# A hybrid decoder layer on one core: the 16 memory-projection tiles placed between gate and z tiles instead of in one block

## The chip, the cores and the metric

The kernel runs on one core of a Trainium2 chip. The metric is the device time of one execution in microseconds, as the median of the runs. TensorE (PE in the profile, its weight loads PEld), VectorE (DVE), ScalarE (ACT), GpSimd (POOL) and the DMA queue of SyncE (SP) each run their own stream of instructions in order and wait for one another by semaphores.

## What is computed

One decoder layer over 512 positions of width 1024, in float32. The normalised input `n` goes through one wide projection; its column blocks feed three branches, and sigmoid gates merge them:

```python
n = rms_norm(h, ln_mix_pre[l])
(da_q, da_k, da_v, dn_q, dn_k, dn_v, dn_z, dn_b, dn_a, ca_q, gate_logits) = [
    n @ wp for wp in jnp.split(w_in[l], SPLIT_IDX, axis=-1)]
y_a = diff_attention(...)      # 8 heads, two softmax maps each
y_b = gated delta rule(...)    # 8 heads, convolution of width 4 on q, k, v
mkv = rms_norm(mem, mem_norm_g[l]) @ w_mem_kv[l]
mk, mv = jnp.split(mkv, 2, axis=-1)
y_c = memory_attention(ca_q, mk, mv)   # 4 heads over 256 memory tokens
proj = jnp.einsum('bsiw,iwd->bsid', ys, w_branch[l])
mixed = jnp.sum(gates * proj, axis=2)
h = h + rms_norm(mixed @ w_out[l], ln_mix_post[l])
```

A squared-ReLU MLP follows. The memory projection (`mkv`) has 256 rows instead of 512.

## The kernel before

**Tiles.** Every projection is cut into weight tiles of 1024 x 128 (512 KB). A float32 product is made of three products of split operands: a tile's weights come into `w_raw` by DMA (L623, three buffers), ScalarE makes the high part `w_hi` (L841), VectorE the low part `w_lo` (L1136), three buffers each. TensorE multiplies them (L1541 to L1543) into one of the two banks of `acc`: 24 matmuls of 512 columns for an ordinary tile, 24 of 256 columns for a memory tile `mk` or `mv`. ScalarE evacuates the bank.

**Slots.** `plan_mixing` (L120) lays the first 104 tiles out over 192 slots. A slot holds half an ordinary tile (12 matmuls) or a whole memory tile, and beside it at most one step of the attention chain (`attn_steps`) and one of the delta chain (`delta_steps`). Every engine walks the same list of slots, so each engine's stream is fixed when the kernel is built. On TensorE the order in a slot is: main half, delta step, attention step. On VectorE: delta step, maxima of an attention map, the low part of the tile three ahead of the one that the slot evacuates, the convolution of that tile, the finish of the tile before, the scaling of the map of two slots before, the norm of an attention output. A low part is thus made only in a slot that evacuates a tile:

```python
                if ev is not None:
                    split_lo(ev + SPL)
```

**The order of the tiles** comes from `ORDER` (L81): groups taken one after the other, each as soon as the step that frees its buffers has been planned, and a gate tile where the next group is not free yet. The groups are `conv` n (q, k, v tiles of delta pair n: `dq`, `dk`, `dv`, two heads each, with a convolution), `mem` (all 16 memory tiles), `cq` n (two tiles of the cross queries), `z` n (two tiles `dz`), `head` n (`aq`, `ak`, `av`). The 24 gate tiles write their sigmoid to HBM, after a pass by GpSimd (L771), and the DMA queue stands until that is done.

**The steps.** Delta pair p (0 to 3; two heads, here called pair p): `dq`, `dk`, `dv` transpose the convolved tiles `conv_o` (L1656) once all six tiles of the pair are finished; `dq` and `dk` are followed by norms on VectorE (L1307 to L1313, `dk` also L1328), while GpSimd fills `d_ET` (L742) after `dk`. Then come transposes, decay, products (`dL`, `dA`), a doubling inversion (`Za`, `Wb`, `Tc`), the scan over four chunks (`sa`, `sb`), whose last step has a norm of the state's output `d_LT` (L1353, L1307 to L1313), and the output `dO` (L1362). Cross head h: `cs` (scores), `ct`, `cv` (values; spilled to HBM by the DMA queue). Attention head h: `av`, `as0` and `as1` (the two maps, L1616; bias and maxima on VectorE, L1271 to L1276, exponentials on ScalarE, L964), scaling of both maps on VectorE (L1287 to L1295), `at` (transposes of the scaled map, L1622), `ap` (value product, L1627; norm of the output `o_a` on VectorE, L1299 to L1303), `ay` (transposes of the output). TensorE starts a step of a chain only when the steps before it in the chain are done on ScalarE and VectorE.

After the 192 slots come the branch projections, the output projection and the MLP, 112 further tiles that the change does not touch.

Of the kernel before, what the change touches and what calls it, by code (L numbers as in the profile page):

```python
# [32 lines left out]
KT = D // P  # L33
# [44 lines left out]

ORDER = [("conv", 0), ("mem", 0), ("cq", 0), ("z", 0), ("conv", 1), ("cq", 1), ("cq", 2), ("cq", 3), ("z", 1),  # L81
         ("head", 0), ("head", 1), ("conv", 2), ("head", 2), ("head", 3), ("z", 2), ("head", 4), ("conv", 3),
         ("head", 5), ("head", 6), ("z", 3), ("head", 7)]

# [1 line left out]
def cover(step):  # L86

    last_state = step[0] == "sb" and step[2] == ST - 1
    return COVER.get("sb_last" if last_state else step[0], 1)


def attn_steps():

    out = [("mv", 0), ("mv", 1)]
    for h in range(HC):
        out += [("cs", h), ("ct", h), ("cv", h)]
    for h in range(HA):
        out += [("av", h), ("as0", h), ("as1", h), ("at", h), ("ap", h), ("ay", h)]
    return out


def delta_steps():

    out = []
    for p in range(HB // 2):
        out += [(k, p, 0) for k in ("dq", "dk", "dv", "dE", "dqT", "dqd", "dkT", "dkb", "dL", "dA", "T1")]
        for lv in range(1, NM):
            out += [("Za", p, lv), ("Wb" if lv < NM - 1 else "Wl", p, lv)]
            if lv < NM - 1:
                out.append(("Tc", p, lv))  # L110
        out += [("dU", p, 0), ("dW", p, 0)]
        for c in range(ST):
            if c:
                out.append(("sa", p, c))
            out.append(("sb", p, c))
        out.append(("dO", p, 0))
    return out


def plan_mixing():  # L120

    attn, delta = attn_steps(), delta_steps()
    def group(kind, n):
        return {"mem": [("mk", j) for j in range(KT)] + [("mv", j) for j in range(KT)],
                "conv": [(k, 2 * n + i) for k in ("dq", "dk", "dv") for i in range(2)],
                "z": [("dz", 2 * n + i) for i in range(2)],
                "cq": [("cq", 2 * n + i) for i in range(2)],
                "head": [(k, n) for k in ("aq", "ak", "av")]}[kind]  # L130

    groups = [group(*g) for g in ORDER]
    gates = [("gate", i * KT + m) for i in (2, 0, 1) for m in range(KT)]
    tiles, slots = [], []
    done = {}
    evac = {}
    need_free = {}
    for p in range(1, HB // 2):
        for k in ("dq", "dk", "dv"):
            for i in range(2):  # L140
                need_free[(k, 2 * p + i)] = ("dv", p - 1, 0)
        for i in range(2):
            need_free[("dz", 2 * p + i)] = ("dO", p - 1, 0)
    for j in range(2 * HC):
        need_free[("cq", j)] = ("mv", 1) if j < 4 else ("cs", j // 2 - 2)
    for h in range(HA):
        for k in ("aq", "ak", "av"):
            need_free[(k, h)] = ("cv", HC - 1) if h < 2 else ("as1", h - 2)
    need_tile = {}
    need_tile[("mv", 0)] = need_tile[("mv", 1)] = ("mv", KT - 1)  # L150
    for h in range(HC):
        need_tile[("cs", h)] = ("cq", 2 * h + 1)
    for h in range(HA):
        need_tile[("av", h)] = ("av", h)
    for p in range(HB // 2):
        need_tile[("dq", p, 0)] = ("dv", 2 * p + 1)
        need_tile[("dO", p, 0)] = ("dz", 2 * p + 1)
    ai = di = 0
    a_next = d_next = 0
    finish = {}  # L160
    todo = list(groups)
    now = []
    half = 0
    slot = 0
    while todo or gates or now or ai < len(attn) or di < len(delta) or finish.get(slot):
        if not now:
            if todo and all(need_free.get(t) is None or need_free[t] in done for t in todo[0][:1]):
                now = list(todo.pop(0))
            elif gates:
                now = [gates.pop(0)]  # L170
        main = ev = None
        if now:
            short = now[0][0] in ("mk", "mv")
            main = (len(tiles), None if short else half)
            if half == 1 or short:
                t = now.pop(0)
                tiles.append(t)
                ev = len(tiles) - 1
                evac[t] = slot
                if t[0] in ("dq", "dk", "dv", "dz"):  # L180
                    finish[slot + 1] = ev
                    evac[t] = slot + 1
            half = 0 if short else half ^ 1
        sa = sd = None
        if ai < len(attn) and slot >= a_next:
            t = need_tile.get(attn[ai])
            if t is None or evac.get(t, slot + 9) < slot:
                sa = ai
                done[attn[ai]] = slot
                a_next = slot + cover(attn[ai])  # L190
                ai += 1
        if di < len(delta) and slot >= d_next:
            t = need_tile.get(delta[di])
            if t is None or evac.get(t, slot + 9) < slot:
                sd = di
                done[delta[di]] = slot
                d_next = slot + cover(delta[di])
                di += 1
        slots.append((main, ev, finish.get(slot), sa, sd))
        slot += 1  # L200
    return tiles, slots, need_free


def plan_tiles():

    tiles, slots, need_free = plan_mixing()
    n_mix = len(tiles)
    tiles = list(tiles)
    for i in (2, 0, 1):
        tiles += [("br", i * KT + m) for m in range(KT)]  # L210
    tiles += [("out", m) for m in range(KT)]
    for half in range(2):
        tiles += [("f1", half * 16 + f) for f in range(16)]
        tiles += [("f2", (2 * half + g) * KT + m) for m in range(KT) for g in range(2)]
    return tiles, n_mix, slots, need_free
# [1720 lines left out]
```

## Time and profile before

| | |
|---|---|
| median of 3 runs | 1498.67 us (1494.84 to 1499.0) |
| the profiled execution | 1497.8 us |
| its span | 1496.0 us, mean granted clock 0.982 |
| TensorE matmul busy | 1432.0 us, 96% of the span |
| TensorE weight loads | 1200.0 us, 80% |
| VectorE busy | 773.1 us, 52% |
| ScalarE busy | 482.7 us, 32% |
| GpSimd busy | 258.7 us, 17% |
| DMA | 142.77 MB, mean 95 GB/s |

The profile is one execution. Matmuls overlap, so a busy TensorE is not one at its peak, and a matmul's length includes the overlap with the next. An idle time stands before the instruction that it delayed, with the engine and tile whose work ended it. The granted clock is a share of 2.4 GHz; its other level is 0.5, 1.2 GHz.

### The profile page before, as it was taken

The numbers are of one execution on the slowest core, as the hardware profiler recorded it, in microseconds if no ns is written. First come the engines' busy times: TensorE is split into PE (matmuls) and PEld (weight loads), VectorE is DVE, ScalarE is ACT, GpSimd is POOL, SyncE is SP. The second block draws the span as 40 slices with busy tenths as digits, with TensorE's granted clock in tenths as the row PEclk, the third lists the DMA queues.
The fourth block names the chain that finished last, engine by engine and source line by source line (L and its number), as shares of the span: only waits on it lengthen the run. The fifth ranks groups of instructions, "written<-read, shape, count | busy, mean of one in ns | idle before, by whom it ended". The sixth has DMA issues, their size and how long they took to land.

```text
span 1496.0 us, 18535 instructions
## 1 busy us (share of the span) xinstructions
PE 1432.0 (96%) x7540; PEld 1200.0 (80%) x7540; DVE 773.1 (52%) x1243; ACT 482.7 (32%) x762; POOL 258.7 (17%) x180
## 2 busy tenths in 40 slices
PE   5879999989999999999899999999979999999998
PEld 5679878768887778888688888888878888888887
DVE  6775236643367676754765334355355533255333
ACT  4334333333243343343343322111243221122221
POOL 2003210005200013100014231223232210022110
PEclk9989999999999999999999999999989999999998
DMA  5243121213111212102312255554412222323221
GB/s 197 69 163 122 64 85 57 85 43 120 57 52 55 78 38 83 62 31 71 106 50 71 92 164 175 189 184 148 168 54 82 97 87 87 111 85 99 97 86 57
DMA packets 46412, 142.77 MB, mean 95 GB/s; under 512 B 4944, under 2 KB 7416, under 8 KB 46328
## 3 DMA queue, kind: packets, MB, share of 16 engines
q1 hardware_dynamic: 46328, 141.59, 28.0%
q8 instruction: 60, 0.98, 0.3%
q14 instruction: 24, 0.20, 0.0%
HBM read 126.88 MB, written 16.27 MB: 96 GB/s over the span
## 4 chain that ended last, share of the span: by engine, by line
PE 82%; DVE 11%; ACT 3%; DMA 2%; issue 2%; SPq 0%; DVEq 0%; POOL 0%; ACTq 0%
PE acc L1541 21%; PE acc L1543 21%; PE acc L1542 21%; PE ps_d L1670 5%; PE ps_a L1616 2%; PE ps_d L1661 2%; DVE conv_y L1232 2%; PE ps_d L1675 2%; DVE w_lo L1136 2%; DMA w_raw<-weights 2%; ACT w_hi L841 1%; PE ps_a L1606 1%; PE ps_a L1627 1%; PE ps_a L1595 1%; PE ps_d L1664 1%
## 5 line engine op out<-in xcount | busy, mean ns | idle before, releaser
L1541 PE MATMUL acc<-n_hi,w_hi 128*128 128x512 f32 (+1 forms) x984 | 399.8, 406 | 6.7 <-DVE n_lo L1161 4.3
L1136 DVE TENSOR_TENSOR w_lo<-w_raw,w_hi 128x1024 fp32r<-128x1024 f32 x200 | 289.0, 1453 | 190.8 <-ACT w_hi L841 190.5
L1542 PE MATMUL acc<-n_lo,w_hi 128*128 128x512 f32 (+1 forms) x984 | 383.8, 390 | 0.0
L1543 PE MATMUL acc<-n_hi,w_lo 128*128 128x512 f32 (+1 forms) x984 | 383.8, 390 | 0.0
L841 ACT CAST w_hi<-w_raw 128x1024 fp32r<-128x1024 f32 x200 | 209.5, 1047 | 249.2 <-PE acc L1543 232.4
L1541 PEld LDWEIGHTS acc<-n_hi,w_hi 128*128 128x128 f32 x984 | 188.6, 192 | 45.4 <-issue 6.4
L1543 PEld LDWEIGHTS acc<-n_hi,w_lo 128*128 128x128 f32 x984 | 187.8, 191 | 41.1
L1542 PEld LDWEIGHTS acc<-n_lo,w_hi 128*128 128x128 f32 x984 | 188.7, 192 | 35.6 <-issue 1.0
L1543 PE MATMUL acc<-h_hi,w_lo 128*128 128x512 f32 x256 | 101.1, 395 | 0.0
L1541 PE MATMUL acc<-h_hi,w_hi 128*128 128x512 f32 x256 | 101.1, 395 | 0.0
L1542 PE MATMUL acc<-h_lo,w_hi 128*128 128x512 f32 x256 | 101.1, 395 | 0.0
L829 POOL TENSOR_TENSOR h_lo<-sq,h_hi 128x512 fp32r<-128x512 f32 x32 | 41.4, 1294 | 234.2 <-DVE h_hi L1472 234.2
L1541 PE MATMUL acc<-y_hi,w_hi 128*128 128x512 f32 x192 | 76.1, 396 | 0.0
L1543 PE MATMUL acc<-y_hi,w_lo 128*128 128x512 f32 x192 | 76.0, 396 | 0.0
L1542 PE MATMUL acc<-y_lo,w_hi 128*128 128x512 f32 x192 | 76.0, 396 | 0.0
L1081 ACT ACTIVATE sq<-relu 128x512 f32<-128x512 f32 x32 | 20.3, 634 | 126.1 <-DVE relu L1470 126.1
L1543 PEld LDWEIGHTS acc<-h_hi,w_lo 128*128 128x128 f32 x256 | 48.0, 188 | 11.7
L1541 PEld LDWEIGHTS acc<-h_hi,w_hi 128*128 128x128 f32 x256 | 48.0, 188 | 11.7
L1542 PEld LDWEIGHTS acc<-h_lo,w_hi 128*128 128x128 f32 x256 | 48.0, 188 | 11.7
L1232 DVE SCALAR_TENSOR_TENSOR conv_y<-conv_x,par,conv_y 128x512 f32<-128x512 f32 x72 | 54.1, 752 | 2.6
L1670 PEld LDWEIGHTS ps_d<-d_TT,d_KTT 128*128 128x128 f32 x384 | 46.5, 192 | 2.3 <-ACT d_KTT L987 0.3
L1541 PE MATMUL acc<-m_hi,w_hi 128*128 128x256 f32 x128 | 39.3, 307 | 9.1 <-DVE w_lo L1136 5.4
(311 smaller groups left out, 2056.5 us busy)
## 6 DMA issues: line engine op xcount, KB each, us to landing
w_raw<-weights SPq DMA_DIRECT2D x200, 512.0 KB, 3.5
gate_scratch<-gate_st SPq DMA_DIRECT2D x24, 256.0 KB, 2.2
g_in<-gate_scratch SPq DMA_DIRECT2D x24, 256.0 KB, 3.8
y_raw<-y_scratch SPq DMA_DIRECT2D x16, 256.0 KB, 3.6
x_tok<-x SPq DMA_DIRECT2D x4, 512.0 KB, 5.3
y_scratch<-y_st SPq DMA_DIRECT2D x4, 512.0 KB, 3.3
y_scratch<-d_ET SPq DMA_DIRECT2D x4, 512.0 KB, 3.2
y_scratch<-y_st SPq DMA_DIRECT2D x8, 256.0 KB, 2.6
```

What stands on the lines that cost most here:

```text
L829: nc.gpsimd.tensor_tensor(h_lo[:, f % 16], sq[:, f % 2], h_hi[:, f % 16].bitcast(F32), ALU.subtract).then_inc(hl_ok, 1)
L841: nc.scalar.copy(w_hi[:, t % SPL], w_raw[:, t % RAW]).then_inc(hi_ready, 1)
L1081: nc.scalar.activation(sq[:, f % 2], relu[:, f % 2], ACT.Square).then_inc(sq_ok, 1)
L1136: V_.tensor_tensor(w_lo[:, t % SPL], w_raw[:, t % RAW], w_hi[:, t % SPL].bitcast(F32), ALU.subtract).then_inc(lo_ready, 1)
L1232: ins = V_.scalar_tensor_tensor(out=y, in0=conv_x[:, n % 2, j:j + S], scalar=par[:, col + j:col + j + 1], in1=y, op0=ALU.mult, op1=ALU.add)
L1541: mm(bank, wh, hi_of(k), start=start and k == 0, stop=False)
L1542: mm(bank, wh, lo_of(k), start=False, stop=False)
L1543: last = mm(bank, wl, hi_of(k), start=False, stop=stop and k == KT - 1)
L1616: last = mm(ps[:, bank_of[q]:bank_of[q] + (q + 1) * P], qkv_T[rows_m, h % 2, 0, q * P:(q + 1) * P], qkv_T[rows_m, h % 2, 1, 0:(q + 1) * P] ...
L1661: last = nc.tensor.transpose(dst[m], src[:, m], ident)
L1670: last = mm(ps_d[:, 0, m * P // 2:(m + 1) * P // 2], a[:, m], halves(b[:, m], c, second), start=True, stop=True)
L1675: last = mm(dst[m], a[:, m], b[:, m], start=True, stop=True)
```

## The change

`ORDER` now takes the memory tiles two by two, as groups `mem` 0 to 7 (`mk` for 0 to 3, `mv` for 4 to 7). Three gate tiles, which before had no place of their own, are named in `ORDER` between them, and the z group of pair 0 as well; cross queries 0 and 1 come after the convolution tiles of pair 1.

```diff
--- before.py
+++ after.py
@@ -78,7 +78,8 @@
 
 
 
-ORDER = [("conv", 0), ("mem", 0), ("cq", 0), ("z", 0), ("conv", 1), ("cq", 1), ("cq", 2), ("cq", 3), ("z", 1),
+ORDER = [("conv", 0), ("mem", 0), ("gate", 0), ("mem", 1), ("mem", 2), ("gate", 1), ("mem", 3), ("mem", 4),
+         ("z", 0), ("mem", 5), ("mem", 6), ("gate", 2), ("mem", 7), ("conv", 1), ("cq", 0), ("cq", 1), ("cq", 2), ("cq", 3), ("z", 1),
          ("head", 0), ("head", 1), ("conv", 2), ("head", 2), ("head", 3), ("z", 2), ("head", 4), ("conv", 3),
          ("head", 5), ("head", 6), ("z", 3), ("head", 7)]
 
@@ -122,15 +123,18 @@
 
 
     attn, delta = attn_steps(), delta_steps()
+    gates = [("gate", i * KT + m) for i in (2, 0, 1) for m in range(KT)]
+    n_early = sum(kind == "gate" for kind, n in ORDER)
     def group(kind, n):
-        return {"mem": [("mk", j) for j in range(KT)] + [("mv", j) for j in range(KT)],
+        return {"mem": [("mk" if n < KT // 2 else "mv", 2 * n % KT + i) for i in range(2)],
+                "gate": gates[n:n + 1],
                 "conv": [(k, 2 * n + i) for k in ("dq", "dk", "dv") for i in range(2)],
                 "z": [("dz", 2 * n + i) for i in range(2)],
                 "cq": [("cq", 2 * n + i) for i in range(2)],
                 "head": [(k, n) for k in ("aq", "ak", "av")]}[kind]
 
     groups = [group(*g) for g in ORDER]
-    gates = [("gate", i * KT + m) for i in (2, 0, 1) for m in range(KT)]
+    gates = gates[n_early:]
     tiles, slots = [], []
     done = {}
     evac = {}
```

The work of each tile and the number of slots, 192, stay. Where things stand, by slot (each ordinary tile takes two):

| slots | main tiles before | main tiles now |
|---|---|---|
| 12-13 | mk 0, mk 1 | mk 0, mk 1 |
| 14-15 | mk 2, mk 3 | gate 16 |
| 16-19 | mk 4 to mk 7 | mk 2 to mk 5 |
| 20-21 | mv 0, mv 1 | gate 17 |
| 22-25 | mv 2 to mv 5 | mk 6, mk 7, mv 0, mv 1 |
| 26-29 | mv 6, mv 7, gate 16 | dz 0, dz 1 |
| 30-33 | cq 0, cq 1 | mv 2 to mv 5 |
| 34-37 | dz 0, dz 1 | gate 18, mv 6, mv 7 |
| 38-49 | convolution tiles of pair 1 | the same |
| 84-95 | convolution tiles of pair 2 | 90-101 |
| 118-129 | convolution tiles of pair 3 | 124-135 |

All delta steps keep their slots (pair 2: `dq` 103, `dk` 105; pair 3: `dq` 148, `dk` 150; last `sb` of pair 1: 98, its `dO`: 101). The attention steps do not: `cs` of cross heads 0 to 3 moves from slots 34, 54, 60, 66 to 54, 60, 66, 72, and every step of the eight attention heads comes six slots later (`as0`, `as1` of head 1 from 91, 94 to 97, 100; `at`, `ap`, `ay` of head 1 from 98, 99, 101 to 104, 105, 107; `as1` and `at` of head 5 from 142, 146 to 148, 152).

First place: ScalarE at the start of the memory tiles, from the last convolution tile of pair 0 on (`conv_x<-conv_y` is its tanh). `mk_T<-acc` evacuates a memory tile, `gate_st<-acc` a gate tile, `w_hi<-w_raw` is the high part of the tile three ahead, `d_Q<-ps_d` and `d_K<-ps_d` are the copies after the q and k transposes. Before:

```order
L841 CAST w_hi<-w_raw 128x1024
L896 COPY mk_T<-acc 128x256
L841 CAST w_hi<-w_raw 128x1024
L927 ACTIVATE conv_x<-conv_y 128x512
L896 COPY mk_T<-acc 128x256
L841 CAST w_hi<-w_raw 128x1024
L990 COPY d_Q<-ps_d 128x1024
L896 COPY mk_T<-acc 128x256
L841 CAST w_hi<-w_raw 128x1024
L896 COPY mk_T<-acc 128x256
L841 CAST w_hi<-w_raw 128x1024
L990 COPY d_K<-ps_d 128x1024
```

Now:

```order
L845 CAST w_hi<-w_raw 128x1024
L900 COPY mk_T<-acc 128x256
L845 CAST w_hi<-w_raw 128x1024
L931 ACTIVATE conv_x<-conv_y 128x512
L900 COPY mk_T<-acc 128x256
L845 CAST w_hi<-w_raw 128x1024
L994 COPY d_Q<-ps_d 128x1024
L924 ACTIVATE gate_st<-acc 128x512
L845 CAST w_hi<-w_raw 128x1024
L994 COPY d_K<-ps_d 128x1024
L900 COPY mk_T<-acc 128x256
L845 CAST w_hi<-w_raw 128x1024
```

Between the copies of q and k there were two evacuations and two high parts, and now there is one of each, of a gate tile.

Second place: VectorE around the last convolution tile of pair 2. `conv_o` is the finish of a convolution, `ps_a<-ps_a,strip` the bias of an attention map, `state` a step of the scan of pair 1, `d_ET<-ps_d,smd,zs` its output, `w_lo` a low part. Before:

```order
L1136 TENSOR_TENSOR w_lo<-w_raw,w_hi 128x1024
L1230 TENSOR_SCALAR conv_y<-conv_x,par 128x512
L1232 SCALAR_TENSOR_TENSOR conv_y<-conv_x,par,conv_y 128x512 x3
L1353 SCALAR_TENSOR_TENSOR state<-state,e_all,ps_d 128x128 x2
L1246 SCALAR_TENSOR_TENSOR conv_o<-conv_x,conv_y 128x512
L1287 RECIPROCAL smd<-smd 128x8
L1288 TENSOR_SCALAR smd<-smd 128x4
```

Then the rest of a scaling, the last state norm of pair 1, an output norm, and right ahead of the norm of q:

```order
L1127 SCALAR_TENSOR_TENSOR smd<-smd 128x4
L1303 TENSOR_TENSOR o_a<-o_a,smd 128x512
L1362 SCALAR_TENSOR_TENSOR d_ET<-ps_d,smd,zs 128x1024
L1136 TENSOR_TENSOR w_lo<-w_raw,w_hi 128x1024
L1307 TENSOR_TENSOR d_SCR<-d_Q 128x1024
L1308 TENSOR_REDUCE smd<-d_SCR 128x8
```

Now:

```order
L1275 TENSOR_TENSOR ps_a<-ps_a,strip 128x3x256
L1276 TENSOR_TENSOR ps_a<-ps_a,strip 128x128
L1278 TENSOR_REDUCE smd<-ps_a 128x1 x4
L1280 TENSOR_SCALAR smd<-smd 128x4
L1250 SCALAR_TENSOR_TENSOR conv_o<-conv_x,conv_y 128x512
L1366 SCALAR_TENSOR_TENSOR d_ET<-ps_d,smd,zs 128x1024
L1140 TENSOR_TENSOR w_lo<-w_raw,w_hi 128x1024
L1234 TENSOR_SCALAR conv_y<-conv_x,par 128x512
L1236 SCALAR_TENSOR_TENSOR conv_y<-conv_x,par,conv_y 128x512 x3
L1250 SCALAR_TENSOR_TENSOR conv_o<-conv_x,conv_y 128x512
L1291 RECIPROCAL smd<-smd 128x8
```

The last `conv_o` stood ahead of the last state norm; now it comes after that norm, after the second map of head 1 and after the output of pair 1, and only the scaling of head 1's maps (L1291 to L1299) lies between it and the norm of q.

Third place: VectorE between the norms of q and k of pair 3 (`d_SCR<-d_K` begins the latter). Before:

```order
L1312 TENSOR_SCALAR smd<-smd 128x8
L1313 TENSOR_TENSOR d_Q<-d_Q,smd 128x1024
L1136 TENSOR_TENSOR w_lo<-w_raw,w_hi 128x1024
L1307 TENSOR_TENSOR d_SCR<-d_K 128x1024
L1308 TENSOR_REDUCE smd<-d_SCR 128x8
```

Now:

```order
L1316 TENSOR_SCALAR smd<-smd 128x8
L1317 TENSOR_TENSOR d_Q<-d_Q,smd 128x1024
L1275 TENSOR_TENSOR ps_a<-ps_a,strip 128x3x256
L1276 TENSOR_TENSOR ps_a<-ps_a,strip 128x128
L1278 TENSOR_REDUCE smd<-ps_a 128x1 x4
L1280 TENSOR_SCALAR smd<-smd 128x4
L1140 TENSOR_TENSOR w_lo<-w_raw,w_hi 128x1024
L1311 TENSOR_TENSOR d_SCR<-d_K 128x1024
L1312 TENSOR_REDUCE smd<-d_SCR 128x8
```

The bias and maxima of head 5's second map now stand between the two norms, and the scaling of its maps comes behind the norm of k. Line numbers of the changed kernel are four higher.

## Rows read from the trace of the kernel before

**Rows 1.** Stretches: start:end, length, busy PE, PEld, DVE, ACT, POOL (instructions), clock, DMA, GB/s

```profile
70.00:106.00 36.00, 24.50 (x168) 23.45 (x169) 30.00 (x51) 13.71 (x23) 2.78 (x1) 0.84 0.35 123
106.00:440.00 334.00, 327.10 (x1923) 280.78 (x1923) 154.88 (x222) 118.59 (x196) 60.48 (x35) 1.00 0.23 79
440.00:550.00 110.00, 103.66 (x546) 84.85 (x545) 77.43 (x160) 43.27 (x82) 1.90 (x1) 0.97 0.20 68
...
700.00:765.00 65.00, 59.53 (x290) 47.97 (x290) 47.77 (x107) 21.88 (x41) 4.17 (x4) 0.95 0.26 90
```

**Rows 2.** The same view: one half projection tile, and one memory tile

```profile
57.78:60.57 2.79, 2.79 (x13) 2.26 (x12) 2.02 (x4) 1.07 (x3) 0.00 (x0) 1.00 0.82 330
118.20:121.14 2.94, 2.94 (x27) 2.94 (x26) 2.36 (x2) 1.65 (x2) 0.00 (x0) 1.00 0.03 11
```

**Rows 3.** TensorE in order of time, memory stretch: start, length, operation, [idle before <-releaser]

```profile
104.31 0.58 PE L1541 MATMUL acc<-m_hi,w_hi 128*128 128x256 f32 x1 [5.39 <-DVE w_lo L1136]
```

**Rows 4.** VectorE in order of time, memory stretch, the norm of k begins

```profile
94.14 2.79 DVE L1307 TENSOR_TENSOR d_SCR<-d_K 128x1024 f32<-128x1024 f32 x1
```

**Rows 5.** TensorE in order of time, its stalls from 200 to 765

```profile
210.33 2.00 PE L1670 MATMUL ps_d<-d_QT,d_KBT 128*128 128x64 f32 x16 [1.44 <-ACT d_QT L985]
...
310.71 1.06 PE L1601 MATMUL ps_a<-cst,p_c 128*128 128x128 f32 x8 [2.70 <-DVE p_c L1284]
...
519.34 2.56 PE L1616 MATMUL ps_a<-qkv_T 64*128 64x512 f32 x8 [1.50 <-ACT p_a L964]
...
535.64 3.41 PE L1664 MATMUL ps_d<-cst,d_ET 128*128 128x128 f32 x16 [2.54 <-issue]
...
718.92 1.87 PE L1622 MATMUL ps_a<-cst,p_a 128*128 128x128 f32 x10 [2.96 <-DVE p_a L1295]
...
739.01 1.07 PE L1656 MATMUL ps_d<-cst,conv_o 128*128 128x128 f32 x8 [2.51 <-issue]
```

**Rows 6.** VectorE in order of time, pair 1's convolutions and pair 2's norms

```profile
466.08 1.23 DVE L1136 TENSOR_TENSOR w_lo<-w_raw,w_hi 128x1024 fp32r<-128x1024 f32 x1 [2.28 <-ACT w_hi L841]
...
469.98 0.60 DVE L1353 SCALAR_TENSOR_TENSOR state<-state,e_all,ps_d 128x128 f32<-128x128 f32 x2
...
507.49 1.22 DVE L1307 TENSOR_TENSOR d_SCR<-d_Q 128x1024 f32<-128x1024 f32 x1 [6.96 <-ACT d_Q L990]
...
513.79 0.96 DVE L1271 TENSOR_TENSOR ps_a<-ps_a,strip 128x768 f32<-128x768 f32 x1
...
521.72 1.23 DVE L1307 TENSOR_TENSOR d_SCR<-d_K 128x1024 f32<-128x1024 f32 x1 [3.55 <-ACT d_K L990]
...
529.07 1.22 DVE L1136 TENSOR_TENSOR w_lo<-w_raw,w_hi 128x1024 fp32r<-128x1024 f32 x1
...
535.55 0.20 DVE L1287 RECIPROCAL smd<-smd 128x8 f32<-128x8 f32 x1
...
539.22 1.22 DVE L1136 TENSOR_TENSOR w_lo<-w_raw,w_hi 128x1024 fp32r<-128x1024 f32 x1
```

**Rows 7.** VectorE in order of time, a state norm and the norm of an output

```profile
706.75 0.61 DVE L1353 SCALAR_TENSOR_TENSOR state<-state,e_all,ps_d 128x128 f32<-128x128 f32 x2 [1.24 <-PE ps_d L1688]
...
713.48 1.63 DVE L1136 TENSOR_TENSOR w_lo<-w_raw,w_hi 128x1024 fp32r<-128x1024 f32 x1
...
728.11 0.68 DVE L1299 TENSOR_TENSOR p_a<-o_a 128x512 f32<-128x512 f32 x1
...
732.55 1.22 DVE L1307 TENSOR_TENSOR d_SCR<-d_Q 128x1024 f32<-128x1024 f32 x1
```

**Rows 8.** TensorE in order of time, a state step and a value product

```profile
705.21 0.39 PE L1684 MATMUL ps_d<-state,d_QDT 128*128 128x128 f32 x2
...
706.11 0.61 PE L1688 MATMUL ps_d<-vnew,d_K 128*128 128x128 f32 x4
...
724.43 2.39 PE L1627 MATMUL ps_a<-v_tok,wT 128*128 128x128 f32 x20
```

**Rows 9.** ScalarE in order of time, exponentials of a map

```profile
517.14 0.37 ACT L964 ACTIVATE p_a<-ps_a,smd 128x128 f32<-128x128 f32 x1 [9.76 <-DVE smd L1276]
```

## The prediction

> **What bounds the kernel now.** I read three views, in this order. First the busy time of stretches: TensorE is busy in 327 of the 334 us from 106 to 440, at a granted clock of 1.00, against 24.5 of 36 us in the stretch from 70 to 106, at 0.84 [rows 1]. So TensorE is the bound, and a change of order can only move the stalls between its instructions. Then the order of time on TensorE, for where it stalls; then the same on VectorE, for what it waits for. The stalls are behind VectorE's long tasks, which stand in a strict queue: the norm of q or k of a delta pair, the convolution tiles, the attention maxima, the rescaling of two maps, the norm of an attention output. A slot's own share of TensorE is 2.79 us for half a projection tile and 2.94 us for a whole memory tile [rows 2], and side steps come on top.
>
> **What the change moves.** Work is neither added nor removed. In slots 12 to 37 memory tiles and half tiles change places one for one. The delta steps keep their slots. Every attention step comes later (cross head 0 by 20 slots, all from the first real head on by 6), and so do the convolution tiles of pairs 2 and 3.
>
> **The memory stretch.** It holds the dearest stall: 5.39 us before the seventh memory tile, mk 6, ended by VectorE's low part of its weights [rows 3]. VectorE was in the norm of k, entered at 94.14 [rows 4], and a low part is made only when a tile is evacuated, three tiles ahead. Before, two prepared memory tiles, mk 4 and mk 5 (2 x 2.94 us), lie behind the k transposes. Now a gate tile takes two slots ahead of those transposes, mk 2 and mk 3 follow them, and mk 4 is the first without a low part, since the gate tile has one evacuation where two memory tiles had two (first pair of listings). TensorE comes to it after 2 x 2.94 us again and waits for the same end of the norm. Nothing ahead of slot 14 is changed, so the waits there stay. I cost the stretch at 0. Its bounds: nothing saved, or all of the 5.39 us and the clock's share behind it (36 x 0.16 = 5.8 us for the whole stretch [rows 1], some 3 to 4 of it here), about 9 us.
>
> **Cross attention.** With head 0 moved away from slots 34 to 38, the 1.44 us stall at 210.33 [rows 5] has lost its cause: in slot 39 the load of a weight tile stood on the DMA queue behind the spill of that head. The same spill now stands in slot 58, where head 1's stood. I take off 1.44; bounds 0 and 1.44. The 2.70 us at 310.71 [rows 5] is a cross head beside the norm of k in slot 60; another head does the same there, so it stays.
>
> **Pair 2 (slots 97 to 107).** Before, the last convolution tile was done seven slots ahead of the q transposes. Now it is one slot ahead (second listings), and pair 1's last state norm and an attention head stand in the same queue. I count both engines from the end of the first map of head 1 on TensorE (slot 97).
> VectorE's costs: maxima 3.2 (513.79 to 517), low part with convolution 3.9 (466.08 to 469.98), scaling of two maps 3.67 (535.55 to 539.22), q norm 6.3 (507.49 to 513.79), k norm 7.35 (521.72 to 529.07) [rows 6]; state norm 6.73 and norm of an output 4.44 [rows 7]. Finishing a convolution is 0.6, or 1.3 where ScalarE's tanh has to come first. TensorE's steps are taken by their rows less the overlap with what follows (a group of eight transposes shows 1.07 and takes 0.85).
> VectorE: maxima 3.2, low part and convolution 7.1, state norm 13.8, finish 14.4, low part and convolution 18.3, maxima 21.5, finish 22.1, output of pair 1 23.3, low part and convolution 27.2, finish 28.5.
> TensorE: half tile 2.8, state step 1.3 [rows 8] so 4.1, half 6.9, half 9.7, second map from 10.1 (after ScalarE's exponentials, 2.2 [rows 5, 9]) to 12.6, half 15.4, output step 16.3, two halves 21.9. The q transposes need the last finished convolution, 28.5: **a stall of 6.6.**
> On from there: transposes 0.85, end 29.4; VectorE scales the maps (32.2), norms q (38.5), makes a low part (39.6). TensorE: half tile, transposed weights (from 32.2, when the maps are scaled), half: 36.0; the k transposes wait for q until 38.5: **2.5.** Then 0.85 and the 2.25 of the value product [rows 8], 41.6, two halves, 47.2. VectorE: copy by ScalarE 40.3, k norm 47.7, with GpSimd's own pass beside it 48.4 (the first instruction took 2.79 beside such a pass [rows 4]), low part 49.5, norm of the output 53.9. The output's transposes wait: **6.7.**
> Gone are the 1.50 and 2.54 of this region [rows 5]; smaller ones on either side I leave out.
>
> **Pair 3 (slots 148 to 152).** The second map of head 5 now stands in q's slot, its scaling in k's. From the end of slot 148's half tile, VectorE: q from 1.85 to 8.2, maxima 11.3; ScalarE: exponentials 13.5, a tanh and k's copy 15.0; VectorE: k norm 22.4, z 23.0, scaling 26.7. TensorE: transposes and second map 3.3, two halves 8.9, k transposes 9.8, two halves 15.4; then the transposes of the scaled map wait until 26.7: **11.3.** Gone are 2.96 and 2.51 [rows 5].
>
> **The clock.** The stretches 440 to 550 and 700 to 765 ran at 0.97 and 0.95, 3.3 us each, with two stalls of 1.50 to 2.96 in each; from 106 to 440 it is 1.00 in spite of 2.70 [rows 1, 5]. So a short stall costs between 0 and 1.6 on top. I take 1.8 for each of the three long ones, by the stretch from 70 to 106 (5.8 for about three stalls), and 0.8 for the short: 6.2 come, 6.5 go. Bounds: 0 and 8. The Trainium skill (TensorE: Matmul & The Clock Gate, Part 1) says that the throttled state is the default and that activity releases it. By that every stall of this size should be followed by half clock, and the four would cost 1.8 each, 7.2, 1 us more than I take; the stall of 2.70 without a fall in the clock speaks against so strict a reading.
>
> **Sum.** New: 6.6 + 2.5 + 6.7 + 11.3 = 27.1, clock 6.2. Gone: 1.44 + 4.04 + 5.47 = 10.95, clock 6.5. Net +15.9 on the profiled execution's 1497.8: 1513.7. The median of the runs is 0.9 higher; with the smaller stalls left out (about 1 us that goes), 1514.
>
> **Rivals.**
> A. The memory stretch also gains. If the interleaving leaves one more tile prepared when VectorE enters the norm of k, up to 9 us go, and the new stalls stay: 1505. For it: this is where the dearest stall is. Against: the slots are as long as before and low parts are made by tile. Chance 0.12.
> B. Faster. The same gain, and VectorE's queue in pairs 2 and 3 catches up. The point that decides: in pair 2 the queue has 28.5 us of work against 21.9 on TensorE; were the state norm done before slot 97's maxima, or the tasks 25% shorter, no stall would be left. Then 1498.7 - 9 - 1.4 = 1488. Against: VectorE was busy in 77 of 110 us there already [rows 1], and the order of its queue is fixed. Chance 0.08.
> C. A wash. The shift by six slots only exchanges stalls of like size: 1498.7 less 1.4, so about 1498. For it: the same kinds of steps met before at a cost of 1.5 to 3 us each. Chance 0.08.
> D. Worse. GpSimd's passes lengthen more of the norms as in [rows 4] (1.6 us each), the convolutions of pair 3 meet the doubling steps, and weight loads wait behind gate stores: 5 to 12 us more, about 1522. Chance 0.12.
> That the change does not do what it says I exclude: the listings show the tiles spread.
>
> **Numbers.** My forecast has 0.60, at 1514, with its own range from the clock (0 to 8) and the cross stall of 1508 to 1518. The range reaches to A below and most of D above: 1504 to 1521. A difference of 0.3%, 4.5 us, is about what a measurement of this kernel can tell from none. Slower by more: forecast, A and D, 0.84 (A at 1505 only just); within: C, 0.08; faster: B, 0.08.
>
> **What would show it.** On TensorE a wait of some 6 us before the q transposes of pair 2, ended by VectorE's or ScalarE's part of the last convolution; one of 2 us before k's; one of 6 us before the transposes of head 1's output; one of 11 us before the transposes of head 5's maps; still some 5 us before the memory tile mk 4, at about 104; nothing at 210. It is wrong if the wait before mk 4 is gone, or if TensorE's idle time from slot 97 to 107 stays under 6 us.

## The result, and the profile after

| | before | after |
|---|---|---|
| median of 4 runs each | 1498.37 us (1494.84 to 1499.0) | 1514.26 us (1510.45 to 1516.73) |
| ratio, with its 95% interval | | 1.0109 [1.0081, 1.0136] |
| the profiled execution | 1497.8 us, span 1496.0 | 1515.32 us, span 1513.5 |
| mean granted clock | 0.982 | 0.975 |
| TensorE busy | 1432.0 us | 1433.9 us |
| VectorE busy | 773.1 us | 776.0 us |

The changed kernel is slower by 15.9 us. No engine has more than 3 us more to do: TensorE's idle time went from 64.0 to 79.6 us (span less busy time), and that is 15.6 of the 17.5 us between the two profiled executions. So the question is where TensorE waits. The same stretches as in [rows 1], of the changed kernel (start:end, length, then busy time of PE, PEld, DVE, ACT and POOL, then clock, DMA, GB/s):

```profile
70.00:106.00 36.00, 25.15 (x148) 22.77 (x148) 28.51 (x49) 12.25 (x20) 3.15 (x2) 0.83 0.36 124
106.00:440.00 334.00, 328.85 (x1940) 283.00 (x1940) 148.17 (x191) 117.98 (x195) 60.14 (x37) 0.99 0.25 84
440.00:550.00 110.00, 94.61 (x497) 78.31 (x496) 80.42 (x172) 37.00 (x66) 1.90 (x1) 0.94 0.18 58
...
700.00:765.00 65.00, 52.47 (x265) 42.69 (x264) 44.80 (x101) 20.18 (x40) 1.90 (x1) 0.89 0.18 61
```

The first stretch, where the memory tiles now stand among gate and z tiles, is as it was: 25.15 us busy against 24.50. Between 440 and 550 TensorE works 9 us less than before, between 700 and 765 7 us less, and both at a lower clock, 0.94 and 0.89 against 0.97 and 0.95. TensorE in order of time shows the single waits (start, length, operation, then in brackets the idle time before it and what ended it):

```profile
103.38 0.58 PE L1545 MATMUL acc<-m_hi,w_hi 128*128 128x256 f32 x1 [5.01 <-DVE w_lo L1140]
...
300.87 1.06 PE L1605 MATMUL ps_a<-cst,p_c 128*128 128x128 f32 x8 [2.70 <-DVE p_c L1288]
...
505.49 1.94 PE L1660 MATMUL ps_d<-cst,conv_o 128*128 128x128 f32 x8 [7.02 <-DVE conv_o L1250]
...
531.40 1.09 PE L1635 MATMUL ps_a<-cst,o_a 128*128 128x128 f32 x4 [7.15 <-DVE o_a L1307]
...
574.88 1.28 PE L1626 MATMUL ps_a<-cst,p_a 128*128 128x128 f32 x10 [1.01 <-DVE p_a L1299]
...
755.51 2.37 PE L1626 MATMUL ps_a<-cst,p_a 128*128 128x128 f32 x10 [12.03 <-DVE p_a L1299]
...
937.45 1.94 PE L1665 MATMUL ps_d<-cst,d_LT 128*128 128x128 f32 x8 [2.80 <-DVE d_LT L1317]
```

They are the q transposes of pair 2 (7.02), the output of head 1 (7.15) and the maps of head 5 (12.03), 26.2 us in all; two more, 1.01 at the maps of a later head and 2.80 before the output step `dO` of pair 3, I had not foreseen. The 2.70 at 300.87 is the one of before at 310.71 [rows 5]. The wait before the memory tile is still there, 5.01 after 5.39 [rows 3], and nothing is left at 210 [rows 5]. The books close: with 0.51 at 736.84 the new waits make 30.5; the stalls that I had as gone make 10.95 [rows 5]; waits under 1 us that vanished, and longer ones that grew shorter, come to 4.3 (0.8 of it in the first 21 us, where both kernels do the same); after TensorE's last matmul the span runs 0.4 longer. That leaves 15.7 for 15.6 of idle time.

VectorE around the last convolution tiles of pair 2 shows the queue that the first of these waits stands behind:

```profile
476.61 0.96 DVE L1275 TENSOR_TENSOR ps_a<-ps_a,strip 128x768 f32<-128x768 f32 x1 [1.93 <-PE ps_a L1620]
...
484.61 1.23 DVE L1311 TENSOR_TENSOR d_SCR<-d_LT 128x1024 f32<-128x1024 f32 x1 [0.51 <-ACT d_LT L987]
...
495.18 0.96 DVE L1275 TENSOR_TENSOR ps_a<-ps_a,strip 128x768 f32<-128x768 f32 x1
...
498.79 1.28 DVE L1366 SCALAR_TENSOR_TENSOR d_ET<-ps_d,smd,zs 128x1024 f32<-128x1024 f32 x1
...
504.65 0.69 DVE L1250 SCALAR_TENSOR_TENSOR conv_o<-conv_x,conv_y 128x512 f32<-128x512 f32 x1 [0.70 <-ACT conv_x L931]
```

From the first maxima of head 1 (476.61) to the last finished convolution (505.34) the queue runs 28.7 us with 1.2 us of waits in it: maxima, the state norm (`d_SCR<-d_LT`), the second map's maxima, the output of pair 1 (`d_ET`), and only then the tile that TensorE needs.

### The profile page after: what moved, and what is told of

It is laid out like the page before. It is cut to its first block, busy times and chain, and to the rows that moved or that the text cites. A ratio compares the mean times of both kernels' runs of the same rounds, so it can differ in the third digit from the quotient of the medians.

```text
span 1513.5 us, 18535 instructions
## 1 busy us (share of the span) xinstructions
PE 1433.9 (95%) x7540; PEld 1204.1 (80%) x7540; DVE 776.0 (51%) x1243; ACT 482.9 (32%) x762; POOL 258.6 (17%) x180
## 3 DMA queue, kind: packets, MB, share of 16 engines
q1 hardware_dynamic: 46328, 141.59, 28.5%
## 4 chain that ended last, share of the span: by engine, by line
PE 80%; DVE 12%; ACT 3%; DMA 3%; issue 1%; POOL 0%; SPq 0%; DVEq 0%; ACTq 0%
PE acc L1545 21%; PE acc L1547 20%; PE acc L1546 20%; PE ps_d L1674 5%; PE ps_d L1665 2%; PE ps_a L1620 2%; DVE conv_y L1236 2%; PE ps_d L1679 2%; DVE w_lo L1140 2%; DMA w_raw<-weights 1%; PE ps_a L1610 1%; ACT w_hi L845 1%; PE ps_a L1631 1%; DMA y_st<-y_scratch 1%; DVE d_SCR L1311 1%
## 5 line engine op out<-in xcount | busy, mean ns | idle before, releaser
L1140 DVE TENSOR_TENSOR w_lo<-w_raw,w_hi 128x1024 fp32r<-128x1024 f32 x200 | 284.7, 1430 | 185.8 <-ACT w_hi L845 185.5
L1546 PEld LDWEIGHTS acc<-h_lo,w_hi 128*128 128x128 f32 x256 | 48.2, 188 | 11.3
L1346 DVE TENSOR_TENSOR d_TT<-d_TT,ps_d 128x512 f32<-128x512 f32 x24 | 16.5, 686 | 68.2 <-PE ps_d L1674 68.2
L746 POOL TENSOR_TENSOR d_ET<-cst,gdec 128x1024 f32<-128x1024 f32 x4 | 7.6, 1895 | 245.3 <-PE ps_d L1660 245.3
```

The costliest lines, as they stand in the source:

```text
L1140: V_.tensor_tensor(w_lo[:, t % SPL], w_raw[:, t % RAW], w_hi[:, t % SPL].bitcast(F32), ALU.subtract).then_inc(lo_ready, 1)
L1546: mm(bank, wh, lo_of(k), start=False, stop=False)
```

## The experiments

Each ran beside the kernel before on the same chip, and its ratio is against those runs. `gates` in `plan_mixing` stays as in the change. Where `ORDER` differs, the new lines that replace the change's first two are shown; `...` marks a cut in the code.

**One: the tiles interleaved, without the shift.** The memory tiles stand apart in slots 12 to 19 as in the change, but cross queries 0 come back ahead of the convolution tiles of pair 1 and the two z tiles are placed singly (a group `zt`), so that every step of cross heads 1 to 3 and of the attention heads has its slot of before (those of cross head 0 come four slots later).

```diff
+ORDER = [("conv", 0), ("mem", 0), ("gate", 0), ("mem", 1), ("mem", 2), ("zt", 0), ("mem", 3), ("mem", 4), ("mem", 5), ("mem", 6), ("mem", 7),
+         ("zt", 1), ("cq", 0), ("conv", 1), ("cq", 1), ("cq", 2), ("cq", 3), ("z", 1),
...
+                "zt": [("dz", n)],
```

> Memory tiles stand between a gate tile and two z tiles as in the change (slots 12 to 19 are the same as there), but all 16 are done by slot 31, so that cross heads 1 to 3 and all attention heads keep the slots they had before. My theory (the loss is the shift by six slots against the delta steps): within 4 us of the kernel before, 1495 to 1502; the wait of about 5 us before mk 4 at about 104 is still there, the waits before the q transposes of pair 2, the output of head 1 and the maps of head 5 are not. Rival (the interleaving itself costs, through gate passes, gate stores and later weight loads): about 1510 to 1515.

Measured: 1497.03 us, ratio 1.0006 [0.9994, 1.0018]. TensorE in order of time:

```profile
104.03 0.58 PE L1546 MATMUL acc<-m_hi,w_hi 128*128 128x256 f32 x1 [5.15 <-DVE w_lo L1141]
...
522.08 2.42 PE L1621 MATMUL ps_a<-qkv_T 64*128 64x512 f32 x8 [1.51 <-ACT p_a L969]
...
538.39 3.65 PE L1669 MATMUL ps_d<-cst,d_ET 128*128 128x128 f32 x16 [2.55 <-issue]
```

The waits of 7 and 12 us are gone and the 1.5 and 2.5 of before are back. To take the memory block apart costs nothing and gains nothing that these runs can tell.

**Two: the shift, without the interleaving.** The 16 memory tiles stand in one block again; the three gate tiles and the z tiles follow, and the cross queries keep the place of the change.

```diff
+ORDER = [("conv", 0), ("mem", 0), ("mem", 1), ("mem", 2), ("mem", 3), ("mem", 4), ("mem", 5), ("mem", 6), ("mem", 7), ("gate", 0),
+         ("gate", 1), ("gate", 2), ("z", 0), ("conv", 1), ("cq", 0), ("cq", 1), ("cq", 2), ("cq", 3), ("z", 1),
```

> All 16 memory tiles in one block as before, then three gate tiles and the z tiles, so that from slot 40 on the order of the change holds, with its shift. My theory: as slow as the change, 1511 to 1518, with waits of about 7 us before the q transposes of pair 2, 7 before the output of head 1, 12 before the maps of head 5. Rival (interleaving costs): 1496 to 1501.

Measured: 1514.57 us, ratio 1.0127 [1.011, 1.0144]. TensorE in order of time:

```profile
103.91 0.58 PE L1545 MATMUL acc<-m_hi,w_hi 128*128 128x256 f32 x1 [5.35 <-DVE w_lo L1140]
...
505.02 1.94 PE L1660 MATMUL ps_d<-cst,conv_o 128*128 128x128 f32 x8 [7.04 <-DVE conv_o L1250]
...
530.96 1.09 PE L1635 MATMUL ps_a<-cst,o_a 128*128 128x128 f32 x4 [7.15 <-DVE o_a L1307]
...
756.27 1.08 PE L1626 MATMUL ps_a<-cst,p_a 128*128 128x128 f32 x4 [12.04 <-DVE p_a L1299]
```

The three large waits of the change, each within 0.02 us, with the memory block in one piece. The two runs together are the main finding: the whole loss belongs to the six slots by which attention steps and convolution tiles moved against the delta steps.

The shift comes from one piece of the edit, the place of cross queries 0 and 1. Behind the convolution tiles of pair 1 they let the last cross head finish in slot 76 in place of 70; the tiles of the attention heads wait for that step, and the planner fills slots 72 to 77 with three gate tiles that stood in 142 to 147 before. No run moves the steps without moving these three tiles, so their part is not told apart by itself; the large waits all end on VectorE tasks of the shifted steps.

**Three: VectorE scales the maps before the norm of k.** In a slot with a `dk` step, VectorE now does the scaling of two maps or the norm of an attention output ahead of its part of the delta step. It concerns slots 105 (a norm) and 150 (a scaling). The two calls go into a function `scale_and_norm`, not shown.

```diff
+                early = sd is not None and DELTA[sd][0] == "dk"
+                if early:
+                    scale_and_norm(n)
...
-                if lagged(n, SCALE_LAG, ("cs", "as1")) is not None:
-                    attn_scale(lagged(n, SCALE_LAG, ("cs", "as1")))
-                if lagged(n, NORM_LAG, ("ap",)) is not None:
-                    attn_scale(lagged(n, NORM_LAG, ("ap",)))
+                if not early:
+                    scale_and_norm(n)
```

> The change, with one thing different: in a slot with the k step of a delta pair VectorE does the scaling of the maps or the norm of an attention output ahead of the norm of k, not behind it. It concerns slots 105 and 150. My theory: the wait for the maps of head 5 falls from 12 to about 2 us and the one for the output of head 1 from 7 to under 1; in their place come waits of 3 to 4 us for k itself at the v transposes. Net 9 to 13 us faster than the change with the clock, 1501 to 1506. Rival (those waits only show a lack of weights or of VectorE's time as a whole): no gain, 1511 to 1518.

Measured: 1506.51 us, ratio 1.0076 [1.0061, 1.0091], 8.1 us under experiment two, which ran on the same chip: by the ratios some 30 to 40% of the loss is back, a little less than the 1501 to 1506 expected. TensorE in order of time:

```profile
503.52 0.87 PE L1667 MATMUL ps_d<-cst,conv_o 128*128 128x128 f32 x3 [7.05 <-DVE conv_o L1250]
...
529.33 1.09 PE L1667 MATMUL ps_d<-cst,conv_o 128*128 128x128 f32 x4 [3.82 <-issue]
...
733.51 1.06 PE L1667 MATMUL ps_d<-cst,conv_o 128*128 128x128 f32 x8 [1.51 <-issue]
...
742.75 2.37 PE L1633 MATMUL ps_a<-cst,p_a 128*128 128x128 f32 x10 [2.57 <-DVE p_a L1299]
...
750.03 1.07 PE L1667 MATMUL ps_d<-cst,conv_o 128*128 128x128 f32 x8 [1.70 <-issue]
```

The wait for the maps of head 5 fell from 12.03 to 2.57: in the change it had been the norm of k in front of them. The wait for head 1's output is gone, but the v transposes now wait 3.82, and around pair 3 new waits of 1.51 and 1.70, and one of 1.32 at 752.42, take up a part as well. The 7 us ahead of q, which stand before the edit's place, did not move. So the order on VectorE is the cause of two of the three waits, and a task that is served first makes the next one late.

**Four: no norm of a state.** The change, but `dO` of pair 1 leaves out the norm of its last state output (this part of the computation is missing), which takes 6.1 us (484.61 to 490.69 in the change) from VectorE's queue ahead of the last convolution tiles.

```diff
-                    if c == ST - 1:
+                    if c == ST - 1 and p != 1:
```

> The change without the norm of the state output of pair 1 (the output of those two heads stays unnormalised): 6.1 us less in VectorE's queue at slot 98. My theory: the wait of 7.0 us before the q transposes of pair 2 falls to 1 or 2, and with part of the clock's loss behind it the time to 1506 to 1510; the waits at head 1's output and head 5's maps stay. Rival (the last convolution is late for another reason, such as ScalarE's tanh or the evacuation): that wait stays above 5, time 1512 to 1516.

Measured: 1511.75 us, ratio 1.0114 [1.0099, 1.013]. The row of TensorE in question:

```profile
501.56 1.26 PE L1660 MATMUL ps_d<-cst,conv_o 128*128 128x128 f32 x8 [3.76 <-DVE conv_o L1250]
```

and VectorE in order of time, where the norm was:

```profile
487.35 1.22 DVE L1140 TENSOR_TENSOR w_lo<-w_raw,w_hi 128x1024 fp32r<-128x1024 f32 x1 [3.03 <-ACT w_hi L845]
```

The wait fell by 3.26 us, about half of the norm, and by less than I had expected. The time missed the expected 1506 to 1510: it is 2.8 us under experiment two on the same chip, and by the ratios not to be told from the change. VectorE got to its next task early and then stood idle for 3.03 us, since ScalarE had yet to make the high part; the two add up to 6.3, the norm. So the state norm in the queue accounts for 3.3 of the 7 us by experiment. For the rest there are the rows of the queue itself, 28.7 us with 1.2 of waits; no run took more out of it. Taking work out pays only until the next engine is late.

**Five: the preload of the branch outputs later.** The wait of 2.80 at 937.45 is not in my forecast. Before, the attention steps ended six slots earlier, and so did the copying of branch outputs (`y_hi<-y_st`, L1393) that follows their end. VectorE of the changed kernel in order of time, beside the last states of pair 3:

```profile
912.41 0.43 DVE L1393 CAST y_hi<-y_st 128x512 fp32r<-128x512 f32 x1 [2.55 <-DMA y_st<-y_scratch]
...
920.39 0.43 DVE L1393 CAST y_hi<-y_st 128x512 fp32r<-128x512 f32 x1 [2.85 <-DMA y_st<-y_scratch]
...
929.49 0.43 DVE L1393 CAST y_hi<-y_st 128x512 fp32r<-128x512 f32 x1 [4.56 <-DMA y_st<-y_scratch]
929.83 0.60 DVE L1357 SCALAR_TENSOR_TENSOR state<-state,e_all,ps_d 128x128 f32<-128x128 f32 x2
930.47 1.91 DVE L1311 TENSOR_TENSOR d_SCR<-d_LT 128x1024 f32<-128x1024 f32 x1
```

VectorE waits 4.56 us for a DMA with the last state's update behind it. The run moves the last three of these copies to slots 189 to 191.

```diff
+            if k >= 5:
+                k = {5: -1, 6: -1, 7: -1, 8: 5, 9: 6, 10: 7}[k]
```

> The change, with three of the eight preloads of branch outputs (a cast on VectorE that waits for its DMA) moved from slots 186 to 188 to slots 189 to 191, behind the last state norm of pair 3. My theory of the 2.80 us wait that I had not counted (VectorE stands in the preloads for their DMA, so the last scan step and its norm are late): that wait falls under 0.5 us, 1 to 4 us faster than the change, 1511 to 1513, if no new wait above 1 us appears at the first branch tile. Rival (the norm is late for another reason, such as GpSimd's passes): the wait stays at 2 us or more, 1513 to 1516.

Measured: 1519.28 us, ratio 1.0133 [1.0112, 1.0154]. The wait before `dO` is gone, so its cause is settled, but the time is no better, by the ratio rather worse (the two intervals overlap), and outside the 1511 to 1513 expected. TensorE in order of time:

```profile
948.89 0.79 PE L1547 MATMUL acc<-y_hi,w_hi 128*128 128x512 f32 x1 [4.70 <-POOL y_lo L771]
```

The first branch tile now waits 4.70 for the low part of its input, on GpSimd. The early copies had kept that wait away, at the price of the other. A wait of 1.29 us before a state step at 925.21 is new as well.

**Six: two z tiles behind the k transposes.** Rival A asked for one more prepared tile when VectorE enters the norm of k. A gate tile does not give it in the change, since it goes ahead of the transposes. Here the two z tiles stand in slots 16 to 19, where mk 4 to mk 7 stood before: behind the k transposes TensorE then has two prepared tiles of 2 x 2.79 us where it had two of 2.94 [rows 2]. Cross queries 0 go back, so that there is no shift from cross head 1 on; the steps of cross head 0 stand as in experiment one.

```diff
+ORDER = [("conv", 0), ("mem", 0), ("mem", 1), ("z", 0), ("mem", 2), ("mem", 3), ("mem", 4), ("mem", 5), ("mem", 6), ("mem", 7),
+         ("gate", 0), ("cq", 0), ("conv", 1), ("cq", 1), ("cq", 2), ("cq", 3), ("z", 1),
```

> The kernel before with the two z tiles of pair 0 in slots 16 to 19, right behind the k transposes, then the other memory tiles, the gate tile and cross queries 0 and 1; from cross head 1 on all slots as before. My theory (the memory stretch stalls because too little prepared work lies behind the k transposes; each ordinary tile is twice as long as a memory tile): the wait of 5.4 us before the seventh memory tile is gone, in its place some 1.5 to 2 us before the v transposes, which need the norm of k themselves; with the clock 4 to 6 us faster than before, ratio 0.996 to 0.9975. Rival (the supply of weights or the count of evacuations sets the pace there, wherever the tiles stand): ratio 0.999 to 1.001, a wait of 5 us in all stays in slots 16 to 20.

Measured: 1490.16 us, ratio 0.9946 [0.9929, 0.9962]: faster than both kernels, and by more than expected. TensorE in order of time, and below it the stretch from 70 to 106:

```profile
75.34 0.55 PE L1545 MATMUL acc<-m_hi,w_hi 128*128 128x256 f32 x1 [3.27 <-issue]
82.00 1.97 PE L1660 MATMUL ps_d<-cst,conv_o 128*128 128x128 f32 x8 [2.22 <-DVE conv_o L1250]
91.60 1.07 PE L1660 MATMUL ps_d<-cst,conv_o 128*128 128x128 f32 x8 [1.38 <-issue]
102.91 1.06 PE L1660 MATMUL ps_d<-cst,conv_o 128*128 128x128 f32 x8 [1.56 <-issue]
```

```profile
70.00:106.00 36.00, 27.56 (x160) 24.42 (x159) 29.85 (x50) 12.09 (x20) 2.77 (x1) 0.91 0.46 153
```

The wait for `w_lo` of [rows 3] has gone; the 1.56 before the v transposes is left in its place, and the k transposes wait 1.38 where it was 0.46. The clock of the stretch is 0.91 for 0.84 [rows 1], and TensorE works 3 us more of the 36. The 1.44 at 210 [rows 5] has gone too, as in experiment one; there is 0.53 at another step. The profiled execution is the slowest of the six (1493.52) and 4.3 us faster than the profiled one of before, 2.8 of it in TensorE's idle and 1.5 in its busy time; why the median gained some 8 us no trace shows.

**Seven: two gate tiles behind the k transposes, in the change.** The same with gate tiles, and with the change's shift kept.

```diff
+ORDER = [("conv", 0), ("mem", 0), ("mem", 1), ("gate", 0), ("gate", 1), ("mem", 2), ("mem", 3), ("mem", 4), ("mem", 5), ("mem", 6), ("mem", 7),
+         ("gate", 2), ("z", 0), ("conv", 1), ("cq", 0), ("cq", 1), ("cq", 2), ("cq", 3), ("z", 1),
```

> The change, with the same tiles in slots 12 to 37 in another order: two gate tiles in slots 16 to 19, right behind the k transposes of pair 0, the other memory tiles in one piece, the third gate tile and the z tiles behind them. The shift of the attention steps is the change's. My theory (two separate effects that add): the 5 us before the fifth memory tile are gone as with the two z tiles, 5 to 9 us faster than the change, 1505 to 1509, and the waits of 7, 7 and 12 us in pairs 2 and 3 stay. Rival (the gain with the z tiles came from the earlier z or later cross queries, not from what stands behind the k transposes): 1512 to 1516.

Measured: 1512.88 us, ratio 1.01 [1.0083, 1.0117], not to be told from the change, and in the range that the rival expected. The `w_lo` wait is gone here too, but the k transposes wait 1.93, the v transposes 1.99, and another wait stands at 118.19. TensorE in order of time:

```profile
103.73 1.06 PE L1660 MATMUL ps_d<-cst,conv_o 128*128 128x128 f32 x8 [1.99 <-issue]
...
118.19 0.98 PE L1665 MATMUL ps_d<-cst,d_Q 128*128 128x128 f32 x7 [2.24 <-ACT d_QT L994]
```

ScalarE, whose `d_QT` ended it, was itself held up, and the DMA queue of SP tells by whom (last fence: queue and line, what it waited for, total, times, longest):

```profile
116.18 1.04 ACT L845 CAST w_hi<-w_raw 128x1024 fp32r<-128x1024 f32 x1 [3.54 <-DMA w_raw<-weights]
117.13 1.00 ACT L994 COPY d_QT<-ps_d 128x1024 f32<-128x1024 f32 x1
```

```profile
SPq L672 <- POOL gate_st L775: 14.7, 2, 7.8
```

The store of a gate tile sits in SP's queue and waits 7.8 us for GpSimd's pass over it, which itself begins only at 108.31, after ScalarE's sigmoid of that tile at 107.63; the weight loads behind it are issued at 109.80, where with z tiles, which store nothing, they went out at 103.97. ScalarE then waits 3.54 for weights, with `d_QT` behind them. So the kind of the tile matters as well as its place. What else is missing of the expected gain, some 1 to 5 us beyond this 2.24, I can't lay to single waits, and it stays open. With it stays open how much of the gain of experiment six comes from what stands behind the k transposes: its later cross head 0 experiment one has too, and gained nothing, but the earlier z tiles have no run of their own.

## Why the prediction was right, point by point

Forecast 1514.0 in 1504 to 1521, measured 1514.26. The mechanism held; some sizes cancelled.

- **Memory stretch, 0.** Right: 5.01 for 5.39, and experiment one shows it apart from all else. My reason (mk 4 meets the end of the norm after the same two memory tiles) is borne out by experiments six and seven, where two prepared tiles of double length do take the wait away.
- **Cross attention, −1.44.** Right: nothing at 210. The reason, the spill on the DMA queue, was not tested by itself; experiment one, which moves that head by four slots, has no stall there either.
- **Pair 2, 6.6 at q.** Right place, 7.02. VectorE's chain, 28.5, took 28.7.
- **Pair 2, 2.5 at k.** It did not come. VectorE finished q 9.9 us after the last convolution, against 10.0 forecast, but TensorE took 9.9 from the q to the k transposes in place of 7.5. It ran at half clock there: the 6.7 us from 503.9 show 5.11 busy at 0.51, so some 2.6 lost. The step that failed is that I charged both, a wait of 2.5 and a clock share of 1.8, where one fills the other.
- **Pair 2, 6.7 at head 1's output.** 7.15.
- **Pair 3, 11.3 at head 5's maps.** 12.03, confirmed by experiment three, which took 9.5 of it off by order alone.
- **Gone: 4.04 and 5.47.** Right, but for 0.51 at 736.84. The small waits that I left out as about 1 us were 4.3.
- **Clock, 6.2 come and 6.5 go.** At the three long stalls it was half of the busy time in their windows: 2.6, 1.6 (3.10 us busy of 6.7) and 2.2 (4.49 busy of 13.7), 6.4 in all; the four of before had 6.5, as I took it. Two more, 1.7 each, stand behind the 2.70 at 300.87 and the 2.80 at 937.45; I had neither. The first comes and goes from one profiled execution to the next (last section) and is not the change's doing. TensorE's busy time grew by 1.9 only, so I can't place this term better than to 2 us or so.
- **Not in the sum at all:** 2.80 before the last `dO` with its clock share, 4.5 us together, and 1.01 at 574.88. (The 2.80 is 1.95 to 2.17 in experiments two, three, four and seven, which keep the early copies.) I had followed the attention steps to their new slots, but not what comes after the last of them. With the 2.5 that did not come and the 3.3 of small waits that went beyond my 1, it nearly cancels; the exact hit of the median is luck to that extent.

Rival A (the memory stretch gains) fell: the change leaves no more tiles prepared than before, and the wait of 5 us stayed. Rival B (faster) rested on the same. Rival C (a wash) is refuted by the result and by experiment two. Of D (5 to 12 us worse still) one part is true, in small: GpSimd beside VectorE at 930. The forecast says that its range held most of D; with D at 1519 to 1526 it held only the lower end.

## What to carry to other kernels

When in-order engines serve two interleaved chains, moving a group of tiles moves the phase of one chain against the other, and that can cost far more than what the group itself does: follow every step that the planner places afterwards, to the last, and add up each engine's queue between two meeting points. A long task ahead of a short one that the bound engine needs is the pattern to look for; reordering by need (experiment three) or more prepared work to cover the long task (experiment six) can win time back, but price what becomes late next: in experiment seven that ate the gain. A half-clock stretch that ends in a wait for another engine can cost nothing more: here 2.6 us of it stood in place of a forecast wait of 2.5.

## What the runs showed of the hardware that was not expected

- **Stalls of one size, with and without half clock.** Before, 2.70 at 310.71 was followed by none in the whole stretch to 440, which shows 1.00 [rows 1, 5]. After, the 2.70 at 300.87 is followed by one: the first row below. It does not go by the order of the tiles. Experiment one has the order of before at this place, and its stall, 2.69 at 309.70, is followed by half clock (second row); experiment two has the order of the change, and its 2.70 at 301.70 is not (third row). The Trainium skill (TensorE: Matmul & The Clock Gate, Part 1) has throttled as the default, released by activity. The strict reading of it in the forecast, that every such stall is followed by half clock, is mine and not the page's: it fits the changed kernel at all six stalls of 2.7 us and more from 106 on, and fails at the two that rows 5 and the third row show. What tells them apart no run here shows.
- **A 12 us wait leaves half clock well behind it.** The last row is the 4.5 us after the wait for head 5's maps: busy throughout at 0.54.

```profile
302.50:305.90 3.40, 3.40 (x10) 2.60 (x10) 0.49 (x1) 0.49 (x1) 0.00 (x0) 0.53 0.00 0
...
309.70:313.10 3.40, 3.40 (x12) 3.03 (x13) 2.12 (x2) 1.45 (x2) 0.00 (x0) 0.50 0.00 0
...
301.70:305.10 3.40, 3.40 (x19) 2.96 (x20) 2.12 (x2) 1.02 (x1) 0.00 (x0) 1.00 0.01 2
...
755.51:760.00 4.49, 4.49 (x17) 4.02 (x18) 1.59 (x2) 1.29 (x2) 0.00 (x0) 0.54 0.02 4
```

- **GpSimd lengthens VectorE.** `d_SCR<-d_LT` at 930.47 took 1.91 us beside a pass of GpSimd (930.00, 1.29 long), and 1.23 without one at 484.61, the same effect as in [rows 4]. The Trainium skill (SBUF — State Buffer, "SBUF: two separate sides") describes a port pair that the two engines share and lock for a whole instruction; of the pass 0.82 us were left when VectorE's instruction began, and 0.68 is what that one took longer, so the trace agrees. In [rows 4] 1.71 us were left of GpSimd's pass (93.07, 2.78 long), and the instruction took 1.57 longer.
